# Retention's norm and gating placed ahead of the stick's exponential and softplus, and an output projection that goes through its weights by row halves

## The reference, cut to what matters

```python
proj = rmsnorm(x) @ w_in                     # 6656 columns: rq rk rv sq sk sv rg ga gb
ret = retention(rope(norm(rq)), rope(norm(rk)), rv)      # 8 heads, 128 wide
ret = group_norm(ret, ret_group_norm) * silu(rg)         # mean, variance, scale, gate
y_a = ret @ w_branch_ret
z = sq @ sk.T * scale                        # stick breaking, 8 heads, strictly causal
log_stay = where(mask, log_sigmoid(-z), 0)   # minus softplus(z)
w = exp(log_sigmoid(z) + sum of log_stay over later keys)
y_b = (w @ sv) @ w_branch_sb
mixed = sigmoid(ga) * y_a + sigmoid(gb) * y_b
x = x + mixed @ w_out
```

## Time and profile before

| | |
|---|---|
| time, median of 3 runs | 1826.9 us (1826.39 to 1827.62) |
| the profiled execution's own time | 1824.48 us |
| its span in the trace | 1822.6 us |
| PE busy | 1762.5 us (97%) |
| POOL busy | 1122.1 us (62%) |
| DVE busy | 992.9 us (54%) |
| ACT busy | 946.8 us (52%) |
| mean granted TensorE clock | 0.987 of full speed |

### The profile page before, as it was taken

One profiled execution on the slowest core, in us unless ns is written; L12 is line 12 of the kernel. 1 busy time (PEld: TensorE's weight loads), 2 busy tenths in 40 slices (PEclk: granted clock), 3 DMA queues, 4 the chain that ended last, 5 costly groups with the idle time before them and its releaser, 6 DMA issues.

```text
span 1822.6 us, 34569 instructions
## 1 busy us (share of the span) xinstructions
PE 1762.5 (97%) x13086; PEld 1555.1 (85%) x13086; DVE 992.9 (54%) x1870; ACT 946.8 (52%) x1398; POOL 1122.1 (62%) x495
## 2 busy tenths in 40 slices
PE   8999999999999999999999999999998999989998
PEld 6877879999999999788888878788888889978887
DVE  5123221992478888444444453355558963565555
ACT  5457543445544444455455555566566832346565
POOL 7955755887888888545544575565575530555654
PEclk9998999999999999999999999999999999999999
DMA  8542433655544444566667634465543411135552
GB/s 307 187 160 93 159 137 144 183 180 181 178 147 140 147 139 142 164 192 193 195 224 239 238 104 168 153 207 195 188 150 111 156 25 73 31 135 192 196 189 81
DMA packets 66465, 292.64 MB, mean 161 GB/s; under 512 B 12992, under 2 KB 13632, under 8 KB 48320
## 3 DMA queue, kind: packets, MB, share of 16 engines
q1 hardware_dynamic: 66368, 291.27, 47.8%
HBM read 289.14 MB, written 1.05 MB: 159 GB/s over the span
## 4 chain that ended last, share of the span: by engine, by line
PE 72%; POOL 11%; DVE 7%; issue 6%; ACT 3%; DMA 1%; POOLq 0%; SPq 0%; DVEq 0%; ACTq 0%
PE bank L981 7%; POOL rows_lo L2755 7%; PE bank L803 6%; PE bank L865 6%; PE bank L1117 6%; PE bank L868 6%; PE bank L1002 6%; PE bank L862 6%; PE bank L985 4%; PE bank L809 4%; PE bank L580 3%; PE bank L581 3%; PE bank L586 3%; PE bank L835 3%; POOL unit_lo L2741 3%
## 5 line engine op out<-in xcount | busy, mean ns | idle before, releaser
L2741 POOL TENSOR_TENSOR unit_lo<-unit_raw,unit_hi 128x2048 fp32r<-128x2048 f32 (+1 forms) x86 | 331.6, 3873 | 163.3 <-ACT unit_hi L1547 135.7
L2755 POOL TENSOR_TENSOR rows_lo<-rows_raw,rows_hi 128x1024 fp32r<-128x1024 f32 x128 | 307.7, 2405 | 89.2 <-ACT rows_hi L1685 50.3
L2782 POOL TENSOR_TENSOR a_lo<-table,a_hi 128x256 fp32r<-128x256 f32 x128 | 178.3, 1393 | 164.2 <-ACT a_hi L1734 164.2
L2395 DVE TENSOR_TENSOR rows_lo<-rows_raw,rows_hi 128x1024 fp32r<-128x1024 f32 x128 | 161.7, 1263 | 188.4 <-ACT rows_hi L1729 188.4
L1729 ACT ACTIVATE rows_hi<-rows_raw 128x1024 fp32r<-128x1024 f32 x128 | 135.6, 1060 | 170.7 <-PE bank L868 170.7
L2813 POOL TENSOR_TENSOR up_lo<-up_raw,up_hi 128x2048 fp32r<-128x2048 f32 x22 | 110.6, 5028 | 161.9 <-ACT up_hi L1790 130.5
L1547 ACT ACTIVATE unit_hi<-unit_raw 128x2048 fp32r<-128x2048 f32 x70 | 134.1, 1916 | 86.1 <-PE bank L586 56.2
L981 PE MATMUL bank<-x_lo_hi,up_hi 128*128 128x512 f32 x640 | 159.8, 392 | 0.0
L809 PE MATMUL bank<-x_lo_hi,rows_lo 128*128 128x256 f32 x1024 | 143.3, 283 | 0.8 <-POOL rows_lo L2755 0.8
L809 PEld LDWEIGHTS bank<-x_lo_hi,rows_lo 128*128 128x128 f32 x1024 | 135.7, 190 | 7.0 <-POOL rows_lo L2755 1.4
L865 PE MATMUL bank<-rows_hi,a_lo 128*128 128x512 f32 x512 | 139.4, 393 | 0.6 <-POOL a_lo L2782 0.6
(11 more groups left out here) (477 smaller groups left out, 3986.4 us busy)
## 6 DMA issues: line engine op xcount, KB each, us to landing
unit_raw<-in_ring SPq DMA_DIRECT2D x74, 1024.0 KB, 4.9
rows_raw<-in_u SPq DMA_DIRECT2D x128, 512.0 KB, 3.5
rows_raw<-in_v SPq DMA_DIRECT2D x128, 512.0 KB, 3.5
up_raw<-in_up SPq DMA_DIRECT2D x44, 1024.0 KB, 5.4
down_raw<-in_down SPq DMA_DIRECT2D x22, 1024.0 KB, 4.9
const<-in_const SPq DMA_DIRECT2D x1, 1792.0 KB, 15.9
X<-in_x SPq DMA_DIRECT2D x2, 512.0 KB, 4.7
unit_raw<-in_ring SPq DMA_DIRECT2D x2, 512.0 KB, 8.3
```

The lines of the kernel that those rows point to most:

```text
L2395: V.tensor_tensor(rows_lo[q][:, :], rows_raw[q][:, :], rows_hi_f[q % 2], ALU.subtract).then_inc(S("v_lo_ready"), 1)
L2741: return nc.gpsimd.tensor_tensor(unit_lo[SLOT_OF[n]][:, w], unit_raw[SLOT_OF[n]][:, w], hi, ALU.subtract)
L2755: nc.gpsimd.tensor_tensor(rows_lo[q][:, :], rows_raw[q][:, :], rows_hi_f[q % 2], ALU.subtract).then_inc(S("u_lo_ready"), 1)
L2782: nc.gpsimd.tensor_tensor(a_lo[q % 2][:, :], table[:, i * ROWS_RING + q, :], a_hi_f[q % 2], ALU.subtract).then_inc(S("a_lo_ready"), 1)
```

## The change

Two independent edits. The first reorders ACT and DVE around the stick's softplus; no operation is added or dropped. On ACT, `rows_squared(0)` and `rows_squared(2)` stand ahead of the Exp and Ln of the two halves. On DVE, `stick_logits` ends at Z; `centred` comes next, then -|z| (`minus_abs`), then `scaled_and_gated(0)` or `(2)`, and only then `softplus`, which waits for Ln. `scaled_and_gated(1)` stands ahead of `decayed(6)`. The second edit goes through `w_out` as half 0 of both column blocks, with `mt 2, 3` turned between them, then half 1 of both; each part is one row half, one column block and one token tile. Banks are given out in the same order.

```diff
+            def wo_part(j, half, c, halves_of=None):
+                n = UNIT_AT["WOUT"] + 2 * j + half
+                hi, lo, wait_hi, wait_lo = parts(n, 4)
...
+                wait_hi()
+                for k in range(4):
+                    wait_drained(pe, ("mt", (4 * half + k) // 2))
+                    mm(o[:, :], at_(mix_hi, k), hi[:, k, :], start=half == 0 and k == 0, stop=False)
+                    mm(o[:, :], at_(mix_lo, k), hi[:, k, :], start=False, stop=False)
+                wait_lo()
+                for k in range(4):
+                    t = mm(o[:, :], at_(mix_hi, k), lo[:, k, :], start=False, stop=half == 1 and k == 3)
...
-            rows("wo", UNIT_AT["WOUT"], 0, mix_hi, mix_lo, arrived=lambda k: wait_drained(pe, ("mt", k // 2)), between=lambda: mixed_turned((2, 3)))
-            rows("wo", UNIT_AT["WOUT"] + 2, 1, mix_hi, mix_lo, tokens_last=True)
+            for j in range(2):
+                for c in range(TC):
+                    wo_outs[j, c] = fill(("wo", j, c))
+                    wo_part(j, 0, c)
+                if j == 0:
+                    mixed_turned((2, 3))
+            for j in range(2):
+                for c in range(TC):
+                    wo_part(j, 1, c)
...
+                if 8 <= j <= 11:
+                    rows_squared(j - 8)
                 if j in (8, 10):
                     act.wait_ge(S("minus_abs_ready"), (j - 6) // 2)
                     step(A(SP[:, :, :], SP[:, :, :], ACT.Exp))
                     A(SP[:, :, :], SP[:, :, :], ACT.Ln, bias=C("ones")[:, 0:1]).then_inc(S("ln_ready"), 1)
-                if 8 <= j <= 11:
-                    rows_squared(j - 8)
...
             for n in range(4):
+                if n == 3:
+                    scaled_and_gated(1)
                 decayed(2 * n)
                 decayed(2 * n + 1)
-                if n == 1:
-                    stick_logits(0)
-                    centred(0)
                 if n == 2:
-                    scaled_and_gated(0)
                     centred(1)
                     stick_weights(0)
-                if n == 3:
-                    scaled_and_gated(1)
-                    stick_logits(1)
-                    centred(2)
+                if n % 2:
+                    half = n // 2
+                    stick_logits(half)
+                    centred(2 * half)
+                    minus_abs(half)
+                    scaled_and_gated(2 * half)
+                    softplus(half)
             stick_out(0)
-            scaled_and_gated(2)
             retention_lo(0)
```

More of the change, by code:

```diff
@@ L769, in _ @@
             rows("yb", UNIT_AT["BSB"] + 1, 1, sb_hi, sb_lo, halves=1, tokens_last=True, between=lambda: mixed_turned((0, 1)))
-            rows("wo", UNIT_AT["WOUT"], 0, mix_hi, mix_lo, arrived=lambda k: wait_drained(pe, ("mt", k // 2)), between=lambda: mixed_turned((2, 3)))
-            rows("wo", UNIT_AT["WOUT"] + 2, 1, mix_hi, mix_lo, tokens_last=True)
+            wo_outs = {}
+            def wo_part(j, half, c, halves_of=None):
+                n = UNIT_AT["WOUT"] + 2 * j + half
+                hi, lo, wait_hi, wait_lo = parts(n, 4)
+                o = wo_outs[j, c]
+                at_ = lambda x, k: x[:, 4 * half + k, c * P:(c + 1) * P]
+                wait_hi()
[6 more added lines that the diff above has]
+                    t = mm(o[:, :], at_(mix_hi, k), lo[:, k, :], start=False, stop=half == 1 and k == 3)
+                if half:
+                    full(("wo", j, c), t)
+                    if c == TC - 1:
+                        release_when_filled(n, ("wo", j, c))
+                elif c == TC - 1:
+                    t.then_inc(S("first_half_done"), 1)
+                    halves_done[0] += 1
+                    release[n] = (S("first_half_done"), halves_done[0])
+            for j in range(2):
[7 more added lines that the diff above has]
+                    wo_part(j, 1, c)
             if upto < 3:
@@ L2161, in stick_logits, with minus_abs, softplus @@
                 step.sync()
+            def minus_abs(half):
                 wait_drained(ve, ("zs", 4 * half + 3))
                 V.scalar_tensor_tensor(SP[:, :, :], Z[:, :, :], -1.0, Z[:, :, :], ALU.mult, ALU.min).then_inc(S("minus_abs_ready"), 1)
+            def softplus(half):
                 ve.wait_ge(S("ln_ready"), half + 1)
```

## The result

| | before | changed |
|---|---|---|
| median of 4 executions each, side by side | 1826.64 us (1822.98 to 1827.62) | 1811.01 us (1809.07 to 1813.76) |
| ratio, 95% interval | | 0.993 (0.9911 to 0.995) |
| profiled execution, its span | 1824.48, 1822.6 us | 1809.52, 1807.6 us |
| mean granted TensorE clock | 0.987 | 0.991 |
| PE busy | 1762.5 us | 1753.9 us |

The change makes the kernel faster, by 0.7% by the ratio in the table and by 0.9% by its two medians.

A forecast was written before the change was run, and what follows sets the result against it. PE, busy 97% of the span, was taken as the bound, with waits for DVE and half clock behind them. 5.16 + 5.42 + 0.85 - 1.4 = 10.0 us off the median 1826.9 gave 1816.9 us, range 1814 to 1822.

The forecast's parts named there:

- The reordering's waits: PE's waits of 3.55 us at `proj 10` and 2.05 at `zs 4, 5` vanish; with slow clock, 5.16 and 5.42 us.
- The new chain to `retention_lo(0)`: Before `proj 12`: this now later work takes 17.9 us, PE waits 1.0 us instead of 1.89; gain 0.85.
- Rival 1: At `proj 12`: the wait for `retention_lo(0)` grows to 2.3 us and the clock falls; 1819.8 us, chance 0.19.
- Rival 2: Table loads following at once cost more: chain 4.1 us longer, PE waits 5.1, clock falls; 1822.6 us, chance 0.05.
- Rivals 3 and 4: Another wait stands behind the bank: 1824 to 1827 us, chance 0.09; or a late root delays `decayed(6)`: 1831, chance 0.03.
- The output projection: The 1.26 us wait goes, but PE idles 2.8 us before turning XN and the clock falls; cost 1.4 us.
- The forecast's 1.1 us for the clock: At the norm behind the output projection: loss from half clock after PE's 2.8 us wait, 1.1 us (0 to 2.7).
- The attention's size: Gain up to PE's turning of `rt 2, 3`: 11.43 us.
- All later stages follow PE and shift with it: After the output projection: the whole 10.0 us gain carries to the end; nothing is paced by something started earlier.
- the sum's transfer to the median of three runs: The profiled 1824.5 us becomes 1814.5; the same 10.0 us taken off the median 1826.9 gives 1816.9.
- The prediction's own sign of being wrong: Late Exp, `proj 12` waiting over 2 us, or the clock falling at places without a wait of 2 us.
- the case of no cost and no new wait: Fast end of the range: neither projection costs anything and the new wait is nil; gain 12.9 us.

The follow-up runs named there:

- the first half alone: The kernel before with the ACT and DVE reordering for the stick's first half only, second half and output projection as before: 1818.38 us, ratio 0.9968.
- before started later: The kernel before plus one write of zeros on DVE ahead of the first norm: 1823.44 us, ratio 0.9997.
- the reordering alone: The changed ACT and DVE order with the output projection of the kernel before: 1813.84 us, ratio 0.9948.
- the projection alone: The kernel before with only the output projection by halves, ACT and DVE order as before: 1825.59 us, ratio 1.0009.
- the change started later: The full change plus one write of zeros on DVE ahead of the first norm: 1813.04 us, ratio 0.994 against the kernel before.
- the change again: The full change measured once more, unchanged, beside the kernel before: 1812.4 us, ratio 0.9937.
- before filled: The kernel before, with PE turning an unread identity tile while it waits at the norms: 1816.09 us, ratio 0.9963.
- Filling: The full change, with PE turning an unread identity tile while it waits at five norms: 1805.84 us, ratio 0.9911 against the kernel before.

## Why the prediction was right, and where it was not

**The reordering's waits.** Right. `centred(0)` runs at 121.43, the drain ends at 126.80 (forecast 127.0), -|z| took 1.87 us (forecast 1.5 to 3.13), Ln ends at 131.1 (forecast 131.35), and `zs 4, 5` find their banks free.

**The new chain to `retention_lo(0)`.** Right. From `decayed(6)` at 150.09 to PE's start at 167.78 it is 17.7 us (forecast 17.9), and PE waits 1.25 (forecast 1.0); 1.24 to 1.28 in the other traces of this order. Rival 1, a fall of the clock at this wait, came true in none of the eight traces: from 130 to 200 us the granted clock is 1.00 in all.

**Rival 2, dearer table loads,** is out: the Exp starts 1.29 us after its load, right behind a root and its own load. The Trainium skill, "ScalarE: Activation LUTs", section "What ACT_TABLE_LOAD costs", adds a drain of 1.38 us to a switch; three loads close behind each other show none here: the load at 125.45 starts 0.02 us after the root ends (125.13 + 0.30). Rivals 3 and 4 are out by the waits that are gone and by the time.

**The output projection.** Mechanism right, size wrong. The wait of 2.95 us (forecast 2.8), the root 0.2 us late (forecast 0.3) and the half clock came as described, and in the profiled pair the edit costs 11.69 - 10.10 = 1.6 us (forecast 1.4). But that is one pair. From turning `rt 2, 3` to the gated mixer's norm the old projection took 900.08 us in before, 900.37 in the first half alone, 900.80 in before started later and 901.39 in the reordering alone. By halves it took 901.69 in the change, 900.84 in the projection alone, 901.00 in the change started later and 900.11 in the change again. The means are 0.2 us apart, and the two orders overlap. The forecast's 1.1 us for the clock took the fall as the edit's own. It came in all four traces by halves, but in two of the four of the old order too.

**The attention's size.** Right for the trace that was read, too small for the program. From PE's arrival at `proj 10` to the turning of `rt 2, 3` the eight traces with the new order take 49.41 to 49.46 us. The four with the old order take 61.06 (before) and 61.03 (before filled), or 63.42 (the projection alone) and 63.49 (before started later). So the reordering is worth 11.6 us there (forecast 11.4) or 14.0, and 12.8 in the mean of these traces. Which of the two it is hangs on how long the half clock lasts after the wait of 2.05 us. Where that was short, the third wait was 2.7 to 2.8 us with a half clock behind it. In the trace that was read it was long and the third wait 1.20. Four traces can't tell how often each comes. The new order has no wait over 1.3 us there.

**The step that failed** is the last one, "All later stages follow PE and shift with it", together with the sum's transfer to the median of three runs. The engines' work does follow. But not all of the clock's falls do. Behind the waits of 2.0 to 3.6 us in the old attention the clock fell in every trace, and behind the one of 2.94 us at the norm within the next 5 us. Behind waits of 1.2 to 1.7 us it fell in one execution and not in another. The prediction's own sign of being wrong, a fall without a wait of 2 us, came true in the reordering alone and in before started later. From the mean clock and the span, the time at half clock is 2 x 0.013 x 1822.6 = 47 us in the trace before and 2 x 0.009 x 1807.6 = 33 in the one after. For before started later it is 62 (clock 0.983, span 1830.2), for the change again 40 (0.989, 1810.8). A quarter to over a third of such time is lost: before's executions at clock 0.991 took 1819.1 us in the mean (2 of them), those at 0.986 took 1825.9 (13), and 2 x 0.005 x 1820 = 18 us of half clock lie between, so 0.37 us each. Filling took it from 40 us to 2 x 0.003 x 1804.0 = 11 and gave 6.6 us, so 0.23 each. The 5 us behind the gated mixer's norm are of this kind: from there to the end the change took 723.6 us in one trace and 728.2 in the other, and before 728.5. Where the idle of the norms is filled, late falls become rare and the two kernels differ by 10.25 us.

**What the gain is.** By all executions, 1824.62 - 1812.3 = 12.3 us; by the change again and the before beside it, 10.9. The landmarks give 11.6 or 14.0 from the attention less 0.2 from the output projection, 11.4 or 13.8. So it is near 11 to 12 us. Of the 5.6 us between the result and the forecast, the output projection's term accounts for 1.2 (0.2 for 1.4) and the attention's for 0.2 to 1.4 on the average. The other 3 to 4 us did not repeat: the four first executions of before lay 2.0 above the median of all 60, those of the change 1.3 below that of all ten. That part is a statement about samples; which late falls made it can't be seen in executions without a trace.

**The range** ended at a gain of 12.9, which it called the case of no cost and no new wait; its own terms add up to only 5.16 + 5.42 + 1.89 = 12.5 for that case. And it assumed one size for each clock term. The 60 executions of before, from 1818.44 to 1829.58 us, show a spread that had no room in it.

## What to carry to other kernels

When one engine serves two consumers in order, put first the short chain that frees banks for the bottleneck, and let the long one (here two table loads, Exp and Ln) run under its work. When weight units are passed in order through a ring, changing the order of products changes which copies stand ahead of the next stage's sums: follow the ring one stage on before counting a removed wait as gain. And take terms that hang on the clock from several executions, or remove them first by filling idle time, before comparing edits worth less than 1%.

## What the runs showed of the hardware, unexpected

- The same wait in the same program may or may not be followed by a half clock: 1.64 us before the second turnings, then 1.09 us for eight in the kernel before and 1.97 in before started later, which is nearly the same program. The Trainium skill, "TensorE: Matmul & The Clock Gate", in Part 1, "The HAM clock gate", calls the cold start run-variable; here this holds in mid-kernel too, at waits of 1.24 and 1.64 us.
- The half clock after the same wait can last 3.5 or 6.5 us. After the 2.05 us before the second scores it ended near 160.7 us in the projection alone and at 164 in before. The shorter one was no gain, because PE then waited longer for DVE and the clock fell again.
- Turnings of an identity tile that nobody reads kept the clock at 1.00 in the stretches shown, and at 0.997 over the whole, and paid for themselves: 6.6 us of 1812, more than the output projection's rearrangement gave in any form.
- The same pass over 1536 elements (-|z|) took 3.13 us in the kernel before and 1.87 in the changed one, where it starts at 122.88 instead of 121.65. This is no chance: 3.13 in all four traces of the old order, 1.86 to 1.88 in all nine that begin with `centred(0)`. In both kernels POOL computes a `unit_lo` until about 123.15, so the slow pass ran beside it for 1.5 us and the other for 0.3. That this is the cause was not tested.
